# A chain of two transformer blocks on one core: the first weight slab in two transfers, two norms by halves of the tokens, and the recurrent mixer's gate multiplied in ahead of its heads' norm

## The reference

```python
h = mlstm_chunkwise(q, k, v, i_pre, log_f)
h = rms_norm(h, head_norm.reshape(MLSTM_HEADS, 1, MLSTM_V_DIM))
h = merge_heads(h).astype(xn.dtype) * jax.nn.sigmoid(og)
return h @ w_out
...
x = x + mixed
x = x + memory_cross_attention(rms_norm(x, xattn_norm[layer]), rms_norm(mem, mem_norm[layer]), ...)
x = x + conv_ffn(rms_norm(x, ffn_norm[layer]), ...)
```

## Time and profile before

| | us |
|---|---|
| median of 3 runs | 2633.13 (2629.62 to 2634.3) |
| profiled execution | 2635.62 |
| its span | 2633.8 |
| TensorE busy in it | 2559.1 (97%) |
| VectorE, ScalarE, GpSimd busy | 1176.8, 528.5, 569.0 |
| mean granted clock of TensorE | 0.979 |

### The profile page before, as it was taken

One profiled execution on the slowest core, in us unless ns is written; L12 is line 12 of the kernel. 1 busy time (PEld: TensorE's weight loads), 2 busy tenths in 40 slices (PEclk: granted clock), 3 DMA queues, 4 the chain that ended last, 5 costly groups with the idle time before them and its releaser, 6 DMA issues.

```text
span 2633.8 us, 35027 instructions
## 1 busy us (share of the span) xinstructions
PE 2559.1 (97%) x13350; PEld 2008.4 (76%) x13350; DVE 1176.8 (45%) x2379; ACT 528.5 (20%) x1149; POOL 569.0 (22%) x494
## 2 busy tenths in 40 slices
PE   8999999999899999999999999999999999999999
PEld 5857899986578998644567767888846864899997
DVE  3024178751413887314646763554400235434750
ACT  1131122111212220212530002222200123212220
POOL 0010135100112540001432321333200004332530
PEclk9989999999899999998999999999999997999999
DMA  6322255743234556210024571222211120243442
GB/s 236 128 96 94 98 216 183 258 174 144 80 128 160 183 220 224 77 72 25 1 77 146 209 271 65 73 87 96 114 50 76 71 107 1 97 154 150 164 180 104
DMA packets 39626, 335.20 MB, mean 127 GB/s; under 512 B 3792, under 2 KB 10064, under 8 KB 22352
## 3 DMA queue, kind: packets, MB, share of 16 engines
q1 hardware_dynamic: 39504, 333.50, 34.3%
HBM read 332.44 MB, written 1.05 MB: 127 GB/s over the span
## 4 chain that ended last, share of the span: by engine, by line
PE 86%; DVE 4%; DMA 4%; POOL 2%; issue 2%; ACT 1%; DVEq 0%; SPq 0%; POOLq 0%; ACTq 0%
PE PS L553 25%; PE PS L752 23%; PE PS L1474 6%; PE PS L1320 5%; PE PS L2407 5%; PE PS L1138 3%; PE PS L2448 3%; PE PS L1486 3%; DMA slot<-in_weights 3%; PE PS L1984 2%; PE PS L1149 2%; PE PS L1161 2%; PE PS L430 1%; PE PS L734 1%; PE PS L2100 1%
## 5 line engine op out<-in xcount | busy, mean ns | idle before, releaser
L553 PE MATMUL PS<-arena,slot 128*128 128x256 f32 x1696 | 372.3, 382 | 17.8 <-DMA slot<-in_weights 12.0
L553 PEld LDWEIGHTS PS<-arena,slot 128*128 128x128 f32 x1696 | 324.4, 192 | 63.6 <-issue 12.2
L553 PE MATMUL PS<-XN,slot 128*128 128x256 f32 (+1 forms) x1248 | 312.6, 411 | 5.0 <-DVE XN L492 5.0
L752 PE MATMUL PS<-SQ,slot 128*128 128x128 f32 (+1 forms) x1984 | 294.6, 301 | 3.8 <-DVE slot L848 3.8
L553 PEld LDWEIGHTS PS<-XN,slot 128*128 128x128 f32 x1248 | 238.0, 191 | 76.7 <-issue 42.5
L752 PEld LDWEIGHTS PS<-SQ,slot 128*128 128x128 f32 x1984 | 268.1, 191 | 17.3 <-DVE slot L848 4.3
L752 PE MATMUL PS<-XN,slot 128*128 128x128 f32 (+1 forms) x1664 | 250.0, 301 | 0.0
L752 PEld LDWEIGHTS PS<-XN,slot 128*128 128x128 f32 x1664 | 226.1, 192 | 10.7
L875 DVE SCALAR_TENSOR_TENSOR arena<-PS,small,arena 128x255 f32<-128x255 f32 (+2 forms) x352 | 174.7, 543 | 50.6 <-ACT arena L819 50.2
L819 ACT ACTIVATE arena<-PS,small 128x256 f32<-128x256 f32 (+1 forms) x176 | 105.2, 616 | 385.6 <-DVE PS L908 245.1
L1474 PE MATMUL PS<-arena,slot 128*128 128x512 f32 (+1 forms) x392 | 157.0, 562 | 3.2 <-POOL arena L2560 2.4
(11 more groups left out here) (245 smaller groups left out, 3468.8 us busy)
## 6 DMA issues: line engine op xcount, KB each, us to landing
slot<-in_weights SPq DMA_DIRECT2D x86, 2048.0 KB, 7.7
arena<-in_mod SPq DMA_DIRECT2D x96, 512.0 KB, 3.5
slot<-in_weights SPq DMA_DIRECT2D x16, 2816.0 KB, 9.7
slot<-in_weights SPq DMA_DIRECT2D x24, 1536.0 KB, 6.8
slot<-in_weights SPq DMA_DIRECT2D x2, 2176.0 KB, 8.9
slot<-in_weights SPq DMA_DIRECT2D x4, 1024.0 KB, 4.7
arena<-in_c SPq DMA_DIRECT2D x3, 1024.0 KB, 10.2
small<-in_small SPq DMA_DIRECT2D x1, 2685.0 KB, 19.1
```

Of the source, the lines that this page charges most:

```text
L553: mm = pe.matmul(o, l, r, start=k == 0, stop=k == len(terms) - 1, skip_group_check=True)
L752: mm = pe.matmul(PS[:, bank, 0:h], lhs[:, k * P:(k + 1) * P], rhs(k), start=first and k == 0, stop=last and k == 3, skip_group_check=True)
```

## The change

1. Slab 0 is loaded by two transfers of 16 tiles each, with a counter of its own for the first; TensorE waits for the second only at tile 16.
2. In the recurrent mixer POOL multiplies OG by O1 as soon as ScalarE has written the head; VectorE waits for all four of these, and the heads' norm, whose squares are still of O1, scales OG instead of O1 into O1. `mixout1` waits for the norm's tiles.
3. `mixout1` with `xnorm1`, and `xo1` with `fnorm1`, go through `add_out_halves`, with a plain add as the read. `xq1`'s first slab (4 tiles of output) is done for the first 128 tokens and then for the other 128; `upa1`'s first block waits for the half that it works on.
4. `half_norms` is now shared with `wo1`, whose instructions stay the same.

```diff
         def next_tiles(pe, n=1):
             g, t = Stream.slab, Stream.tile
-            if t == 0:
+            if g == 0 and t == 0:
+                pe.wait_ge(sems["landed_first"], 16)
+            elif t == 0 or (g == 0 and t == 2 * DK):
                 pe.wait_ge(sems[f"landed{g % 2}"], 16 * (g // 2 + 1))
...
             def read(dve, m, g):
+                if gate is None:
+                    dve.tensor_tensor(X[:, m, part[g]], PS[:, m % 4, part[g]], X[:, m, part[g]], ALU.add)\
+                        .then_inc(*tick(VD, s, "read", m, g))
+                    return
...
+        TOKEN_HALVES = [slice(0, P), slice(P, T)]
+
+        def half_norms(s, gain, before, shift=None):
+            return [[f"{s}{g}", norm_x(f"{s}{g}", X, XN, gain, after_out_half(before, g), [0], shift=shift, span=(g * P, P))]
+                    for g in range(2)]
+
+        def tensor_first_halves(pe, s, ready):
+            w = next_tiles(pe, 4 * DK)
+            for g in range(2):
+                for m in range(4):
+                    if g == 0 and m % 2 == 0:
+                        claim(pe, m // 2)
+                    c = TOKEN_HALVES[g]
+                    for k in range(DK):
+                        if m == 0:
+                            pe.wait_ge(*of(*ready(k, g)))
+                        a = (m * DK + k) * P
+                        mm = pe.matmul(PS[:, m // 2, (m % 2) * T:(m % 2 + 1) * T][:, c], w[:, a:a + P], XN[:, k, c],
+                                       start=k == 0, stop=k == DK - 1, skip_group_check=True)
+                    if g and m == 1:
+                        mm.then_inc(*tick(TD, s, "job", 0))
+                    elif g and m == 3:
+                        finish(mm, s, "job", 1)
...
-                           outs=[(O1[:, 2 * h + i, :], O1[:, 2 * h + i, :], col("head_norm", 2 * h + i), None,
+                           outs=[(O1[:, 2 * h + i, :], OG[:, 2 * h + i, :], col("head_norm", 2 * h + i), None,
...
+                def gpsimd_gate(pool):
+                    for h in range(4):
+                        pool.wait_ge(*of("lstmatt", "out", h))
+                        pool.wait_ge(*of("lstmog", "read", h, 0))
+                        o = OG[:, 2 * h:2 * h + 2, :]
+                        pool.tensor_tensor(o, O1[:, 2 * h:2 * h + 2, :], o, ALU.mult).then_inc(*tick(GD, "lstmgated", h))
+                add(gpsimd=gpsimd_gate, vector=lambda d: d.wait_ge(*of("lstmgated", 3)))
...
-                add_out("mixout1", lambda k: O1[:, k, :], lambda k: ("lstmgated", k // 2), DK, [0])
+                x_halves = half_norms("xnorm1", lambda m, g: col("xattn_norm1", m), "mixout1")
+                add_out_halves("mixout1", lambda k, c: O1[:, k, c], lambda k: [("headnorm", "out", k // 2, k % 2)], DK, range(4, DK),
+                               None, x_halves, (0, DK - 1), TOKEN_HALVES)
...
+                def tensor_xq(pe, q_jobs=q_jobs):
+                    tensor_first_halves(pe, "xq1", lambda k, g: (f"xnorm1{g}", "out", 0, k))
+                    tensor_linear(pe, "xq1", q_jobs[2:], 2)
...
+                f_halves = half_norms("fnorm1", lambda m, g: col("ffn_norm1", m), "xo1")
+                add_out_halves("xo1", lambda k, c: O1[:, k, c], lambda k: [("xatt1", "out", k // 2)], DK, range(4, DK),
+                               None, f_halves, (0, DK - 1), TOKEN_HALVES)
...
-            add_ffn(f"a{l}", "a", [0], lambda m, g, s=s: [(s, "out", 0, m)], aside=(
+            add_ffn(f"a{l}", "a", [0], lambda m, g, l=l: [("fnorm0" if l == 0 else f"fnorm1{g}", "out", 0, m)], aside=(
...
-                load(g, len(table[g][1]), piece(g))
+                if g == 0:
+                    sp.dma_start(slots[0][:, 0:2 * DK * P], piece(0)[:, 0:2 * DK * P]).then_inc(sems["landed_first"], 16)
+                    sp.dma_start(slots[0][:, 2 * DK * P:4 * DK * P], piece(0)[:, 2 * DK * P:4 * DK * P])\
+                        .then_inc(sems["landed0"], 16)
+                else:
+                    load(g, len(table[g][1]), piece(g))
```

More of the change, by code:

```diff
@@ L267, in two_blocks @@
         for n in ("tensor_done", "scalar_done", "vector_done", "gpsimd_done",
-                  "landed0", "landed1", "mod_landed0", "mod_landed1", "mod_landed2", "mod_landed3", "late_landed0", "late_landed1", "loaded_c", "loaded_x", "loaded_mem", "loaded_ctx", "loaded_small", "loaded_rest",
+                  "landed0", "landed1", "mod_landed0", "mod_landed1", "mod_landed2", "mod_landed3", "late_landed0", "late_landed1", "loaded_c", "landed_first", "loaded_x", "loaded_mem", "loaded_ctx", "loaded_small", "loaded_rest",
                   "conv_done", "mod_done", "stored"):
@@ L1538, in after_out_half @@
             return [[(s, "read", m, g), (s, "read", m + 1, g)] for m in range(0, DK, 2)]
+        TOKEN_HALVES = [slice(0, P), slice(P, T)]
[19 more added lines that the diff above has]
+                        finish(mm, s, "job", 1)
+            for j in range(2):
+                lend(j, (s, "read", j, 0))
         def after_out(s, segs, gate):
@@ L1898, in two_blocks @@
                 add(vector=lambda d, keys=keys: reads_linear(d, VD, "vector", "memk3", [keys]))
[L1900 to L1907, removed]
-                add_out("mixout1", lambda k: O1[:, k, :], lambda k: ("lstmgated", k // 2), DK, [0])
+                x_halves = half_norms("xnorm1", lambda m, g: col("xattn_norm1", m), "mixout1")
+                add_out_halves("mixout1", lambda k, c: O1[:, k, c], lambda k: [("headnorm", "out", k // 2, k % 2)], DK, range(4, DK),
+                               None, x_halves, (0, DK - 1), TOKEN_HALVES)
             s = f"xnorm{l}"
-            units = norm_x(s, X, XN, lambda m, g, l=l: col(f"xattn_norm{l}", m), after_out(f"mixout{l}", [0], None),
-                           [0])
+            q_jobs = feature_jobs(xn, at_out(s, DK), 8, lambda j, bank: [
+                ("scalar", act_op(Q1[:, 2 * j:2 * j + 2, :], copies(None, bank), scale=-0.0625))])
             if l == 0:
+                units = norm_x(s, X, XN, lambda m, g: col("xattn_norm0", m), after_out("mixout0", [0], None), [0])
                 add_norm_within(s, units, "memk0", memory_keys(0))
+                add_linear("xq0", q_jobs)
             else:
-                add_norm(s, units)
-            add_linear(f"xq{l}", feature_jobs(xn, at_out(s, DK), 8, lambda j, bank: [
-                ("scalar", act_op(Q1[:, 2 * j:2 * j + 2, :], copies(None, bank), scale=-0.0625))]))
+                def tensor_xq(pe, q_jobs=q_jobs):
+                    tensor_first_halves(pe, "xq1", lambda k, g: (f"xnorm1{g}", "out", 0, k))
+                    tensor_linear(pe, "xq1", q_jobs[2:], 2)
+                add(tensor=tensor_xq, scalar=lambda a, q_jobs=q_jobs: reads_linear(a, SD, "scalar", "xq1", q_jobs))
             add_attention(f"xatt{l}", cross_units(l), [(f"xq{l}", "read", 3, 0)] + (
@@ L2580, in two_blocks @@
             else:
[L2581 to L2584, removed]
+                norms = half_norms(s, lambda m, g, l=l: GAIN[:, l, 1, m, g:g + 1], f"wo{l}", mod_col(l, 3))
                 add_out_halves(f"wo{l}", lambda k, c: Y[:, k, c], lambda k, l=l: [(f"merge{l}", "merged", k)], DK,
-                               range(4, DK), gate1, norms, (0, DK - 1), part)
+                               range(4, DK), gate1, norms, (0, DK - 1), TOKEN_HALVES)
                 add_ffn(f"b{l}", "b", segs, lambda m, g, s=s: [(f"{s}{g}", "out", 0, m)], gate2)
```

5 lines of the change are left out of this document (2 added, 3 removed).

## The result

The changed kernel took 2614.12 us (median of 4 runs, 2611.73 to 2616.46) beside 2631.38 for the kernel before on the same chip: ratio 0.9933, 95% interval 0.9916 to 0.9951. Forecast: 2620.1, with a range from 2614.5. Its profiled execution took 2612.25, span 2610.4.

A forecast was written before the change was run, and what follows sets the result against it. TensorE, 86% of the last-ending chain, was taken as the bound, so gains lie where it idles or runs slowly. 2.7 + 1.8 + 4.7 + 3.8 = 13.0 off 2633.13 gives 2620.1; own range 2617 to 2623.5, wider 2614.5 to 2626.5.

The forecast's parts named there:

- Part 1: At the start, loading slab 0 in two transfers lets TensorE begin earlier: gain 2.7 us, bounds 0 and 4.9.
- The rival that both halves land together: Pieces of slab 0's two transfers interleave, so splitting gives 0: gain 10.3, time 2622.8 us; chance 0.12.
- Part 2: Gate multiplied ahead of the heads' norm, so the run of 58 matmuls in `mixout1` starts earlier: gain 1.8 us.
- the clock still falls: In the heads' norm hole TensorE idles and drops to the lower clock; otherwise 2.2 us more would be won.
- Its last wait there is 3.28 us, for POOL's multiply: Reading of the old profile: TensorE's last wait in the heads' norm hole was for POOL's multiply of the gate.
- Part 3: `mixout1` and `xnorm1` by halves, through `xq1`: 59.1 us against 63.8, smaller hole, clock shouldn't fall; gain 4.7 us.
- Part 4: `xo1` and `fnorm1` by halves, into `upa1`: gain 3.8 us, bounds 0 and 5.2.
- The bracket 5.2 − 0.9 − 0.5: 5.2 us won to the end of `upa1`'s first block, less 0.9 for `c` and 0.5 for the second slab.
- Rows of `c`: In `upa1`, `c` is issued when `xo1` ends and lands 10.2 us later, delaying ScalarE and VectorE: stall 0.9 us.
- The second slab: In `upa1` it lands some 0.5 us later relative to TensorE: stall 1.6 for 1.14, costing another 0.5.
- The slower rival: Weight loads of 191 ns set the pace of half-width matmuls: 17 us slower, about 2650 us; chance 0.02.
- 2620.1 on the median's: Forecast for the whole kernel: 13.0 us off the kernel before, on the scale of its median 2633.13 us.

The follow-up runs named there:

- `a_c_early`: Changed kernel with the transfer of `c` issued one slab earlier in both up projections; 2612.46 us, ratio 0.9922 to the kernel before.
- `p2_gate`: Kernel before with only the gate multiplied in ahead of the heads' norm, `mixout1` left whole; 2631.94 us, ratio 1.0006.
- `p3_xnorm`: Kernel before with only `mixout1`, `xnorm1` and `xq1` by halves; 2625.63 us, ratio 0.9979.
- `p1_slab`: Kernel before with only the first slab loaded in two transfers; 2628.18 us, ratio 0.9989.
- `b_again`: Kernel before, run again without an edit; 2629.87 us, ratio 0.9993.
- The two fillers: Filler matmuls behind the sums of `xnorm1` and `fnorm1`, kernel before (2630.08 us, 0.9990); and in the heads' norm hole, changed kernel (2617.23 us, 0.9941).
- `a_hole`: Changed kernel with six filler matmuls in the hole of the heads' norm, within `mixout1`; 2617.23 us, ratio 0.9941 to the kernel before.
- `a_third`: Changed kernel run once more without an edit, on the same chip as `a_hole`; 2615.59 us, ratio 0.9941 to the kernel before.

## Why the prediction was right in its places and too small in its sum

**Part 1, 2.7.** Measured 2.1 to 2.6 in the traces, 2.7 and 2.6 by the means. Right, by its mechanism: the first half landed 7.67 after its issue, 2.09 before the whole slab did (2.7 forecast). The rival that both halves land together is out.

**Part 2, 1.8.** The start of the run moved by 1.67, and "the clock still falls" held. What I left out is that the time won is partly run off at the lower clock: alone it gives 0.24 us up to `xo1` and nothing in the runs. Beside the halves it gives 1.0 or 2.0 in the stretch, and here the runs show 5.0 (give or take 1.6). It was the one part whose worth depends on the others. The added multiplies were hidden as forecast: POOL's fourth ends at 693.93, VectorE's norm starts at 694.46. "Its last wait there is 3.28 us, for POOL's multiply" was a wrong reading: without that multiply the wait is as long, and it is VectorE's pace.

**Part 3, 4.7.** From the start of the 58 matmuls to the end of `xq1`: 757.74 + 13.83 − 711.86 = 59.7, where I had 59.1 (and 63.8 before). Each term can be read: 8.93 for 80 records of half width, idle 1.01 where I had 1.32, 14.29 and 13.83 as forecast. The first 52 records took 14.26 for 11.2 at the full rate, so 3.0 went to the low clock where the 27.16 that I started from holds 2.1 (27.16 less 116 times 0.216); with the shorter idle that makes the 0.6 too many, and it is the effect that undid part 2 alone. The clock stayed at 1.00 through the hole.

**Part 4, 3.8.** From the start of `xo1` to the down projection: 177.1 before, 171.7 after, 5.4 won, more than the bound of 5.2. The bracket 5.2 − 0.9 − 0.5 went like this. Up to the end of the first block: 38.3 us, 5.5 won for 5.2. Rows of `c`: transfer 10.95 for 10.2, stall 1.3 for 0.9, right in kind, and the trace of `a_c_early` confirms the cause. The second slab: this step failed. I had a stall of 1.6 for the 1.14 of before; there was none, so the term is +1.1 where I had −0.5. POOL got its quarter at 843.40 and TensorE never came to wait for it. That stall is 1.14 us in both traces of the kernel before, 1.28 in `p2_gate` and 1.59 in `p3_xnorm`, but none in `p1_slab`, all with the same code there, and none in any trace with `fnorm1` by halves. What decides it stays open.

**The slower rival** (weight loads as the pace of half-width matmuls) is out: 0.1116 us a record in all new stretches.

**The sum.** By parts I missed little: 13.0 forecast, 13.6 in the touched stretches. The 6.0 us between 2620.1 and 2614.1 are made up of four pieces. The base: "2620.1 on the median's" rests on 2633.13, a median of 3 runs; 97 runs have 2631.0, so 2.1 too much. The terms: 0.6. The four runs against the mean of 22 (2614.6): 0.5. That leaves 2.8 that the runs gain outside the touched stretches (16.5 by the means, give or take 1.3, less 13.6), and that I had at nothing: I took all that the diff doesn't touch as constant ("`wo1`'s own lines do what they did"). And the range took 4.7 us from the runs shown without asking what makes them differ.

**The step that failed** is the sum's. Its base was too high: on 2631.0 the same working gives 2618.0 with a range from 2612.4, and the measured 2614.1 lies inside. Its largest mis-sized term is the second slab's wait, −0.5 where the traces have +1.1. And the 2.8 us outside the touched stretches had no term at all; the runs show them, their cause stays open.

**What is shown of the 2.8, and what stays open.** The runs of one kernel differ mostly with the clock: among 93 runs of the kernel before the span is 2.1 us shorter for each 0.001 that the run's mean granted clock is higher (correlation −0.71), among 22 of the changed kernel 2.0 (−0.88). How long TensorE runs at the lower level is drawn anew in sparse stretches that nobody touched. Summed over a trace it is 109 and 98 us in the two of before, and 84, 94, 91 and 88 in the four of after. Of these, 20.5 and 6.8 lie in the touched stretch, which leaves 89 and 78 outside it before and 77 to 87 after: no difference. The waits of `L848`'s kind in untouched up projections show none either: 2.7 and 0 us in the two of before, 1.1 to 1.5 in the four of after. The mean granted clocks of the runs (0.9806 and 0.9833, a time at the lower level of 102 and 87 us) say the same: nearly all of the drop of 15 is the 13.7 of the touched stretch. So the 2.8 does not come from there, and I can't place it. The traces' rest (2335.8 on average of two, 2332.1 of four) leans the same way but scatters more than that. The runs put it beside the gate's move: 5.0 for 2.0 in the stretch, with mean granted clocks of 0.9818 and 0.9833, of which 2.0 us for 0.001 would make 3.0 in all. But `p2_gate` has the same move and wins nothing outside its stretch. That later stages are only shifted by the change isn't the cause, since `b_again` has the short stages as well. Nor is it one chip: beside the kernel before on the same chip the four sets gained 17.5, 16.9, 18.3 and 16.0 us. Chance alone is unlikely, not excluded (2.8, give or take some 1.4). The two fillers, whose runs give 2.4 and 4.1 less than their stretches (1.0 and 2.9 less against the runs on the same chip), point the other way and belong to the same open question.

The Trainium skill (TensorE: Matmul & The Clock Gate, HAM oscillation — how this bites in real kernels) prices a fall at half of the time spent throttled, and says that idle TensorE brings it about. Here the traces agree in place: `a_hole` keeps the clock by being busy, and in `a_third` 52 records lose 2.8 us to a low stretch of 6.8, of which 1.2 lie in the hole and 5.6 in the run; half of 5.6 is 2.8.

## What to carry to other kernels

Where one stage feeds the next through a norm, splitting the last tiles and the norm by halves of the tokens was worth 4 to 6 us a place here in the traces, because it removes the idle time and the clock's fall together; a single multiply taken out of a hole was worth nothing alone that the runs could show, since the rest ran at the lower clock. When a stage gets faster, look at transfers that are issued at its end: `c` became the next wait, and issuing it one slab earlier removed that wait. Make the sum against a mean of many runs, and compare the touched stretches in several traces, before a difference of two spans is explained: of 23.4 us here 10.2 lay in code that did not change.

## What the hardware showed that I had not expected

- Untouched, identical stages differ by up to 5 us from execution to execution, where the work is sparse, with a granted clock of 0.60 against 0.69 over one such stretch of 38 us; 29 of 41 blocks of 200 records repeat within 0.1 us in all eighteen traces. Up projections differ by single waits of 1.1 to 1.6 us. In the 38 us TensorE is busy for 35, but with few, slow records:

```profile
2180.88 1.22 PE L2035 MATMUL PS<-arena,small 128*128 128x256 f32 x2
2182.04 2.07 PE L2216 MATMUL PS<-rms,small 8*128 8x512 f32 x4
2184.04 1.22 PE L2035 MATMUL PS<-arena,small 128*128 128x256 f32 x2
```

- Keeping TensorE busy with filler held the clock in each trace (27.88 for 29.82, 11.49 for 14.25). Of the 3.7 us of the one stretch the runs give 1.3 or 2.7, by what they are set against, and none of the other's 2.7, though six runs can't exclude it.
- The wait for a slab that was issued when its slot came free is not a fixed number: 0 to 1.6 us with the same code in that place.
